# Plain fp32 gate panels in the recurrent mixer, the last output panel pair summed in PSUM, output tiles 4 to 6 in one column sum, last residual and stores by pairs

## The reference

```python
def recurrent_mixer(h, w_in, conv_w, conv_b, w_a, b_a, w_x, b_x, lam, w_out):
    gate, xr = jnp.split(h @ w_in, 2, axis=-1)
    gate = jax.nn.gelu(gate, approximate=True)
    xr = causal_conv(xr, conv_w, conv_b)       # 4 taps along the tokens
    return (rg_lru(xr, w_a, b_a, w_x, b_x, lam) * gate) @ w_out
```

## Time and profile before

| | us |
|---|---|
| median of 3 runs | 3352.14 |
| lowest and highest | 3350.11, 3352.18 |
| profiled execution, its own time | 3345.8 |
| its span (first to last instruction) | 3344.1 |
| TensorE busy | 3141.9 (94%) |
| VectorE busy | 2293.2 (69%) |
| ScalarE busy | 1737.4 (52%) |
| mean granted TensorE clock | 0.971 of full speed |

### The profile page before, as it was taken

One profiled execution on the slowest core, in us unless ns is written; L12 is line 12 of the kernel. 1 busy time (PEld: TensorE's weight loads), 2 busy tenths in 40 slices (PEclk: granted clock), 3 DMA queues, 4 the chain that ended last, 5 costly groups with the idle time before them and its releaser, 6 DMA issues.

```text
span 3344.1 us, 43867 instructions
## 1 busy us (share of the span) xinstructions
PE 3141.9 (94%) x17560; PEld 2704.5 (81%) x17560; DVE 2293.2 (69%) x2787; ACT 1737.4 (52%) x2100; POOL 4.3 (0%) x21
## 2 busy tenths in 40 slices
PE   9998999998899999999998899999787999997798
PEld 8876888887688888888886788888675888886687
DVE  7667575857486776676857576775865675857674
ACT  6455554645464653555545555555443554544553
POOL 0000000000000000000000000000000000000000
PEclk9998999999899999999999899999897999998899
DMA  6542354553255454454553245454330454553353
GB/s 231 189 151 101 132 191 168 192 190 134 90 177 191 174 189 163 162 190 171 191 180 126 81 173 190 175 189 175 140 126 1 170 191 168 192 192 120 115 188 125
DMA packets 75354, 534.73 MB, mean 160 GB/s; under 512 B 8480, under 2 KB 8608, under 8 KB 10784
## 3 DMA queue, kind: packets, MB, share of 16 engines
q1 hardware_dynamic: 75168, 532.07, 44.6%
HBM read 530.99 MB, written 1.05 MB: 159 GB/s over the span
## 4 chain that ended last, share of the span: by engine, by line
PE 79%; DVE 10%; ACT 6%; DVEq 3%; issue 1%; DMA 0%; SPq 0%; ACTq 0%
PE pp L1886 35%; PE pp L1887 18%; PE pm L1886 8%; PE pp L2010 4%; PE pm L1887 4%; PE pp L1909 4%; DVE wlo L1667 3%; PE pp L1911 2%; ACT whi L1500 2%; ACT corr L1572 1%; DVEq L382 1%; DVE mix L1829 1%; DVE mix L385 0%; DVE h L1725 0%; PE pp L1405 0%
## 5 line engine op out<-in xcount | busy, mean ns | idle before, releaser
L1886 PE MATMUL pp<-xs,whi 128*128 128x512 f32 x4912 | 1737.9, 399 | 27.6 <-DVE tsum L1744 25.8
L1667 DVE TENSOR_TENSOR wlo<-raw,whi 128x2048 fp32r<-128x2048 f32 x482 | 1101.8, 2289 | 425.2 <-ACT whi L1500 424.6
L1887 PE MATMUL pp<-xs,wlo 128*128 128x256 f32 x4912 | 1372.0, 279 | 0.0
L1886 PEld LDWEIGHTS pp<-xs,whi 128*128 128x128 f32 x4912 | 931.1, 190 | 256.3 <-issue 39.5
L1500 ACT ACTIVATE whi<-raw 128x2048 fp32r<-128x2048 f32 x482 | 918.9, 1910 | 283.5 <-DMA raw<-weights 282.6
L1887 PEld LDWEIGHTS pp<-xs,wlo 128*128 128x128 f32 x4912 | 933.1, 190 | 0.7 <-issue 0.2
L1572 ACT ACTIVATE corr<-pp 128x512 f32<-128x512 f32 x356 | 211.7, 595 | 564.0 <-PE pp L1887 538.4
L1744 DVE TENSOR_TENSOR tsum<-pp,corr 128x512 f32<-128x512 f32 x343 | 236.4, 689 | 295.1 <-ACT corr L1572 294.5
L1886 PE MATMUL pp<-hs,whi 128*128 128x512 f32 x1120 | 395.8, 394 | 0.0
L1886 PE MATMUL pm<-hs,whi 128*128 128x512 f32 x1120 | 393.0, 392 | 0.0
L1887 PE MATMUL pm<-hs,wlo 128*128 128x256 f32 x1120 | 313.1, 280 | 0.0
(11 more groups left out here) (335 smaller groups left out, 2390.9 us busy)
## 6 DMA issues: line engine op xcount, KB each, us to landing
raw<-weights SPq DMA_DIRECT2D x503, 1024.0 KB, 4.8
raw<-weights SPq DMA_DIRECT2D x8, 256.0 KB, 7.2
h<-x_by_feature SPq DMA_DIRECT2D x4, 256.0 KB, 6.2
out<-h SPq DMA_DIRECT2D x4, 256.0 KB, 2.5
vec<-vectors SPq DMA_DIRECT2D x1, 264.0 KB, 2.9
lamrow<-diff_lambda SPq DMA_DIRECT2D x1, 128.0 KB, 11.5
skiprow<-ssm_d SPq DMA_DIRECT2D x1, 8.0 KB, 12.3
```

What stands on the lines that cost most here:

```text
L1667: v.tensor_tensor(wlo[:, slot, :], raw[:, slot, :], whi[:, slot, :].bitcast(F32), ALU.subtract).then_inc(sem("weights_lo"), 1)
L1886: mm(bank, whi[:, slot, c:c + P], x_k, start=start, stop=False)
L1887: return mm(bank[:, 0:T], wlo[:, slot, c:c + P], x_k[:, 0:T], start=False, stop=stop)
```

## The change

Four things change. (1) In FFN and hybrid sublayers the products for output tiles 6 and 7 go by `summed_product`: three matmuls of 256 columns that add whi*xhi, whi*xlo and wlo*xhi in one PSUM column range. ScalarE then squares and scales all last tiles from PSUM. (2) VectorE folds tiles 4, 5 and 6 before one column sum. (3) The recurrent mixer reads its gate panels and the block product as whole panels in plain fp32. Order of panels: four x, one gate, block, three gate, four out. TensorE's gate panels read `R_IN`, h scaled by the gain (in y), and their output is multiplied by the norm factor on the way out. ScalarE does the convolution's tap with bias. (4) The last residual is made by pairs of tiles, and the stores follow these.

```diff
             subs.append(dict(kind=REC, gain=g + 2, segs=[
-                Segment("rec_in_first", 6), Segment("rec_block", 1, reads=0), Segment("rec_in_last", 2), out_proj("rec_out")]))
+                Segment("rec_x", 4), Segment("rec_gate_first", 1, reads=0, whole=True), Segment("rec_block", 1, reads=0, whole=True),
+                Segment("rec_gate_last", 3, reads=0, whole=True), out_proj("rec_out")]))
         subs.append(ffn(9 + 2 * l, g + 4))
...
+        R_GATE, R_X, R_CONV, R_R, R_I, R_A, R_A2, R_TH = (mix[:, b] for b in range(8))
+        R_IN = y
+        def rec_gates(buf, t):
+            return pm[:, 2 * buf:2 * buf + 2, :].rearrange("p b (e t) -> p (b e) t", e=2)
+            def first_tap(p):
+                act.wait_ge(sem("rec_x"), p + 1)
+                for k in (2 * p, 2 * p + 1):
+                    e = nc.scalar.activation(R_CONV[:, k, :], R_X[:, k, :], ACT.Identity, bias=vec[:, k, VEC_REC_CONV_B:VEC_REC_CONV_B + 1],
+                                             scale=vec[:, k, VEC_REC_CONV_W + 3:VEC_REC_CONV_W + 4])
+                e.then_inc(sem("rec_tap"), 1)
...
+                first_tap(p - 1)
+                if p == 1:
+                    for k in range(KD):
+                        e = nc.scalar.activation(R_IN[:, k, :], h[:, k, :], ACT.Copy, scale=vec[:, k, s["gain"]:s["gain"] + 1])
+                    e.then_inc(sem("rec_in"), 1)
+            read_out(xseg, s, after_first=lambda: rstd(rpre[:, :], 2 * s["n"]), hook=hook)
+            first_tap(3)
+            nc.scalar.preload_act_table_set("sigmoid_and_others")
+            for t in range(2):
+                for buf, (dst, bias_row) in enumerate(((R_R, VEC_REC_BA), (R_I, VEC_REC_BX))):
+                    if (t, buf) == (1, 1):
+                        act.wait_ge(sem("panel_done"), s["segs"][2].g0 + 1)
+                    else:
+                        act.wait_ge(sem("rec_gates"), 2 * t + buf + 1)
+                    for k in range(4):
+                        c = 4 * t + k
+                        e = nc.scalar.activation(dst[:, c, :], rec_gates(buf, t)[:, k, :], ACT.Sigmoid,
+                                                 bias=vec[:, c, bias_row:bias_row + 1])
+                    e.then_inc(sem("rec_sigmoid"), 1)
+            halves = (slice(0, 4), slice(4, 8))
+            for t, q in enumerate(halves):
+                act.wait_ge(sem("rec_log_a"), t + 1)
+                nc.scalar.activation(R_A[:, q, :], R_R[:, q, :], ACT.Exp).then_inc(sem("rec_a"), 1)
+                nc.scalar.activation(R_TH[:, q, :], R_R[:, q, :], ACT.Tanh).then_inc(sem("rec_tanh"), 1)
+            nc.scalar.preload_act_table_set("sqrt_and_others")
+            for t, q in enumerate(halves):
+                act.wait_ge(sem("rec_one_minus_a2"), t + 1)
+                nc.scalar.activation(R_TH[:, q, :], R_TH[:, q, :], ACT.Sqrt, scale=-1.0).then_inc(sem("rec_sqrt"), 1)
+            nc.scalar.preload_act_table_set("gelu_apprx_tanh_and_others")
+            for p in range(4):
+                act.wait_ge(sem("rec_gate_out"), p + 1)
+                q = slice(2 * p, 2 * p + 2)
+                nc.scalar.activation(R_GATE[:, q, :], R_GATE[:, q, :], ACT.Gelu_apprx_tanh).then_inc(sem("rec_gelu"), 1)
+            read_out(s["segs"][4], s)
+        def dve_rec(dve, s, read_out, split):
+            r2 = rpre[:, :].rearrange("p (a t) -> p a t", a=1).to_broadcast([P, 2, T])
+            def conv(p):
+                dve.wait_ge(sem("rec_tap"), p + 1)
+                for j in (2, 1, 0):
+                    d = 3 - j
+                    for k in (2 * p, 2 * p + 1):
+                        v.scalar_tensor_tensor(R_CONV[:, k, d:T], R_X[:, k, 0:T - d], vec[:, k, VEC_REC_CONV_W + j:VEC_REC_CONV_W + j + 1],
+                                               R_CONV[:, k, d:T], ALU.mult, ALU.add)
+                    dve.drain()
+                v.memset(small[:, 1:2], 0.0).then_inc(sem("rec_conv"), 1)
+            def hook(p):
...
+                if p >= 2:
+                    conv(p - 2)
...
+            read_out(s["segs"][0], s, lambda p: R_X[:, 2 * p:2 * p + 2, :], hook=hook)
+            conv(2)
+            conv(3)
+            def gate_in(p):
+                g = s["segs"][1].g0 if p == 0 else s["segs"][3].g0 + p - 1
+                dve.wait_ge(sem("panel_done"), g + 1)
+                v.tensor_tensor(R_GATE[:, 2 * p:2 * p + 2, :], in_banks[p % 2][:, :, 0:T], r2, ALU.mult).then_inc(sem("rec_gate_out"), 1)
+            gate_in(0)
+            for t, q in enumerate(halves):
+                dve.wait_ge(sem("rec_sigmoid"), 2 * t + 1)
+                for k in range(4 * t, 4 * t + 4):
+                    e = v.tensor_scalar(R_R[:, k, :], R_R[:, k, :], rec_col[:, 4, k:k + 1], None, ALU.mult)
+                e.then_inc(sem("rec_log_a"), 1)
+                dve.wait_ge(sem("rec_sigmoid"), 2 * t + 2)
+                v.tensor_tensor(R_I[:, q, :], R_I[:, q, :], R_CONV[:, q, :], ALU.mult)
+            gate_in(1)
+            for t, q in enumerate(halves):
+                dve.wait_ge(sem("rec_a"), t + 1)
+                v.tensor_tensor(R_A2[:, q, :], R_A[:, q, :], R_A[:, q, :], ALU.mult)
+                dve.drain()
+                dve.wait_ge(sem("rec_tanh"), t + 1)
+                v.scalar_tensor_tensor(R_TH[:, q, :], R_A2[:, q, :], 1.0, R_TH[:, q, :], ALU.add, ALU.mult
+                                       ).then_inc(sem("rec_one_minus_a2"), 1)
+            gate_in(2)
+            for t, q in enumerate(halves):
+                dve.wait_ge(sem("rec_sqrt"), t + 1)
...
+            gate_in(3)
+            for p in range(4):
+                dve.wait_ge(sem("rec_gelu"), p + 1)
+                q = slice(2 * p, 2 * p + 2)
...
+            read_out(s["segs"][4], s)
...
+            def gate_panel(g, p):
+                slot = g % SLOTS
+                pe.wait_ge(sem(f"raw_landed_{slot}"), landings(g))
+                if p < 2:
+                    pe.wait_ge(sem("panel_out"), s["segs"][1].r0 + p - 1)
+                else:
+                    pe.wait_ge(sem("rec_gate_out"), p - 1)
+                for ft in range(2):
+                    for k in range(KD):
+                        c = k * PC + ft * P
+                        e = nc.tensor.matmul(in_banks[p % 2][:, ft, 0:T], raw[:, slot, c:c + P], R_IN[:, k, :], start=(k == 0),
+                                             stop=(k == KD - 1))
+                e.then_inc(sem("panel_done"), 1)
+            pe.wait_ge(sem("rec_in"), 1)
+            gate_panel(s["segs"][1].g0, 0)
+            block = s["segs"][2].g0
+            pe.wait_ge(sem(f"raw_landed_{block % SLOTS}"), landings(block))
+            for t in range(2):
+                for buf in range(2):
+                    if t:
+                        pe.wait_ge(sem("rec_sigmoid"), buf + 1)
+                    for k in range(4):
+                        if buf == 0 and k % 2 == 0:
+                            pe.wait_ge(sem("rec_conv"), 2 * t + k // 2 + 1)
+                        c = (buf * KD + 4 * t + k) * P
+                        e = nc.tensor.matmul(rec_gates(buf, t)[:, k, :], raw[:, block % SLOTS, c:c + P], R_CONV[:, 4 * t + k, :],
+                                             start=True, stop=True)
+                    e.then_inc(sem("panel_done" if t and buf else "rec_gates"), 1)
+            for p in range(1, 4):
+                gate_panel(s["segs"][3].g0 + p - 1, p)
+            pe.wait_ge(sem("rec_gate_out"), 4)
+            out_products(s, R_A, lambda k: pe.wait_ge(sem("rec_gated"), k // 2 + 1))
...
             for pair in range(4):
                 q = slice(2 * pair, 2 * pair + 2)
-                sp.wait_ge(sem("h_ready"), KD * (len(subs) - 1) + 2 * pair + 2)
+                sp.wait_ge(sem("h_ready"), KD * (len(subs) - 1) + pair + 1)
                 sp.dma_start(out[:, q, :], h[:, q, :]).then_inc(sem("result_stored"), 16)
...
                         act.wait_ge(sem("panel_done"), seg.g0 + seg.panels)
-                    if seg.whole:
-                        src = banks[:, t, 0:T]
-                    else:
-                        nc.scalar.activation(corr[:, 1, t * T:(t + 1) * T], banks[:, t, T:2 * T], ACT.Copy).then_inc(sem("last_corr"), 1)
-                        act.wait_ge(sem("last_out"), 2 * s["closes_with_y"] + t + 1)
-                        src = y[:, k, :]
+                    src = banks[:, t, 0:T]
                     nc.scalar.activation(sq[:, k, :], src, ACT.Square).then_inc(sem("last_squares"), 1)
...
                     fold_squares(0, 1)
                 else:
-                    fold_squares(4, 5)
+                    add_squares(4, 5)
+                    dve.wait_ge(sem("last_squares"), 2 * s["n"] + 1)
+                    fold_squares(4, 6)
...
                 output_squares(s, 1)
-                if not seg.whole:
-                    for t, k in enumerate((KD - 2, KD - 1)):
-                        dve.wait_ge(sem("last_corr"), 2 * s["closes_with_y"] + t + 1)
```

(71 more changed lines are left out.)

91 lines of the change are left out of this document (18 added, 73 removed).

## The result

The changed kernel took 3306.97 us (median; 3302.77 to 3310.58) against 3351.12 for the kernel before in the same comparison: ratio 0.9869, 95% interval 0.9852 to 0.9886. Timed once more as an experiment it gave 0.9862 (0.9847 to 0.9878). The forecast was 3305 from 3352.1, a ratio of 0.9859. The profiled execution has a span of 3305.2 us, 38.9 less than before.

The account below looks back on a forecast made before the run. TensorE, busy 94% of the span, was taken to bound the kernel, with VectorE bounding the recurrent mixer. Terms -32.4 (mixer), -16.9 (closings), -1.1 (residual), +3 (matmuls) sum to -47.4 us: 3305 from 3352.14, range 3299 to 3311.

Parts of the forecast that it names:

- The mixer (-32.4): Recurrent mixer: output projection starts 30.3 us earlier, and runs 2.1 us shorter without the lower clock.
- the layout: Recurrent mixer's new order on the old time axis, engine by engine: output projection at about 3081.55 in place of 3111.81.
- The clock part of 2.1 us: Recurrent mixer's output projection: 28.0 us at the full clock in place of 30.1, since the hole before it shrinks.
- The rival of a dropping clock: Recurrent mixer: small TensorE holes still drop the clock; with a late ScalarE about +8 us, 3313; chance 0.20.
- The closings (-16.9): Ends of sublayers: both parts together shorten the stretch from first to last sum of output squares, 16.9 us in all.
- The 0.63: Sublayer closings: forecast us from the first sum of output squares to the last, in 17 closings.
- the 1.87: FFN and hybrid closings before the change: us from first to last sum of output squares, in 12 closings.
- -0.23 in 5 of them, -1.1 us: Closings with whole output panels: one column sum less moves the last sum from +0.86 to +0.63.
- the 1.23: FFN closings: forecast us saved in a stretch from one closing to the next, before the added matmuls' cost.
- The added matmuls (+3): FFNs and hybrid mixer: 560 products with one more matmul each add 3 us in the sum, with ends 0 and +6.
- The rival of loads in line: Summed products: the 560 added weight loads are not hidden and cost 106 us, giving 3408; chance 0.03.
- The last residual (-1.1): Kernel's end: sixteen passes become eight by pairs, 5.65 us against 6.75, fourth store earlier; 0 if stores queue.

Follow-up runs that it names:

- experiment 7: The kernel before with 39 small, unused matmuls of ones in the 18 us hole ahead of the recurrent mixer's output projection; ratio 0.9993 (0.9984 to 1.0003).
- experiment 2: The kernel before with only the recurrent mixer's plain fp32 gate and block panels added; 3319.5 us, ratio 0.9907 (0.9894 to 0.992).
- experiment 3: The changed kernel's closings, column sum and last residual on the old recurrent mixer; 3335.2 us, ratio 0.9952 (0.9939 to 0.9964).
- experiment 4: The kernel before with the 512-column matmul of 2136 down products made as two of 256 columns; 3358.62 us, ratio 1.0021 (1.0012 to 1.003).

## Why the prediction was right, point by point

- **The mixer (-32.4).** Measured 31.9 from first matmul to the first sum of squares in the profiles of the changed kernel, 30.6 in the profile of part 3 alone, 31 (27 to 36) timed alone. Each step of the layout held: after the earlier start of 5.13 us is taken off, gate panels 1 to 3 were to start at 3053.2 and did at 3053.44; the scans' end, gate read 3 and the projection's start were off by at most 0.4 (3076.81 against 3076.4). The clock part of 2.1 us is shown by experiment 7. That it comes in full is in part luck: the hole of 2.5 us left the clock at 1.00 in both profiles of the changed kernel, but behind the same hole the profile of experiment 2 has the lower clock for 3.4 us, and the mixer took 1.3 us more. The rival of a dropping clock was priced at 2.1 us and as much again, and where it came true it cost less.
- **The closings (-16.9).** The 0.63 is 0.64; the 1.87 is gone in 12 closings, the last gives 0.9, and VectorE's second fold is in time; the one closing of 0.60 has its first sum 0.04 later behind the last product than the others, since the fold came late there, and its last sum is not later for it. The term that was mis-sized is "-0.23 in 5 of them, -1.1 us": it is -0.22 + 0.11 = -0.11 each, some 0.6 us, since a sum that had to wait runs 0.1 us longer. In the FFNs that loss was there before and after, and the 1.23 stands.
- **The added matmuls (+3).** The FFN stretch fell by 0.87 in the first profile (190.27 to 189.40) and by 0.94 in experiment 3, not 1.23, so 44 products cost 0.29 to 0.36, 0.007 to 0.008 each, 3.7 to 4.6 us for 560; by experiment 4, 0.003 to 0.005 each, 1.8 to 2.9 us. Rows 6 gave +4. No row or run shows why the term should be 3 rather than that, and the summed products themselves came out at the 4. Why the form of experiment 4 is the cheaper one stays open. The rival of loads in line fell to experiment 4.

  The rule of the Trainium skill weighed in the prediction ("TensorE: Matmul & The Clock Gate", "The mechanism" and "LDWEIGHTS (loading the stationary operand)") would have made experiment 4 dearer by 2136 loads at 107 ns, 229 us as an estimate; the measured 7 us do not agree. "The mechanism" also lets a load into the background weight buffer go ahead of matmuls in flight; no run here can show that.
- **The last residual (-1.1).** 6.75 to 5.56, and the end follows it by 3.0 us as before, so the stores did not queue: -1.2.
- **The sum.** 47.4 forecast, 44 and 46 measured. The profile's span gave 38.9 only. Most of what lacks is the hybrid mixer's stretch, which was to be 1.2 us shorter and came out 3.9 longer, at a mean clock of 0.88 against 0.90 before. The other mixers that the change left alone do not repeat either: the first HGRN-2 stretch took 184.7 to 187.6 us over the ten profiles, and the second is 2.8 to 2.9 shorter in every kernel with part 1, where its closings explain 1.2. The rest of that stays open. Three sublayers also start 0.3 to 0.4 us later after their closing (4.08 to 4.16 in place of 3.8 or 3.7), about 1 us in all. In each of the three one instruction of the chain behind the last sum, on VectorE or ScalarE, starts 0.34 to 0.45 us late without a wait that the profile shows. They are the same three in every kernel with parts 1 and 2. What holds them stays open.

## What to carry to other kernels

Read the last waits of a stage in the order in which they end: a second saving (one column sum less) is worth nothing, or less, until the first (the add through y) is gone. When a stage is bound by another engine, matrix work that is dearer for TensorE but needs no preparation is a gain, as long as it is laid under that engine's busy time; and reads of such work belong behind what is ready in the other engine's queue. Cost a change by stages, close to close: here most FFN stretches repeat to 0.1 us where whole executions differ by 10. Stretches in which the clock falls repeat less well, so compare the clock's low time before the length.

## What the runs showed of the hardware

A 512-column fp32r matmul made as two of 256 with a load each costs 3 to 8 ns more, though a load's record is 188 ns long. A pair of fp32 matmul instructions that had to wait for its operand runs 0.32 us start to start in place of 0.22. The hybrid mixer, whose matmuls fill 259 of 307 us, took 311 to 320 us over the ten profiles, with the mean granted clock from 0.87 to 0.91; the same code got 0.88 in one execution and 0.91 in the next. The same hole of 2.5 us of TensorE left the clock at 2.4 GHz in two profiles, and in a third the clock was at 1.2 GHz for 3.4 us right behind it.
